# Attention in a decoder step: the second four heads of each block are normalised on GpSimd instead of ScalarE

## What is computed

```python
s = jnp.einsum('bnqhgd,bnkhd->bnhgqk', qb, kb).astype(jnp.float32) * (HEAD_B ** -0.5)
s = jnp.where(valid[None, :, None, None], s + bias[None], NEG_INF)
m = jnp.maximum(s.max(-1), sink)
p = jnp.exp(s - m[..., None])
p = p / (p.sum(-1) + jnp.exp(sink - m))[..., None]
return jnp.einsum('bnhgqk,bnkhd->bnqhgd', p, vb.astype(jnp.float32))
```

## Time and profile before

| | |
|---|---|
| median of 3 runs | 1639.69 us (1639.18 to 1644.08) |
| the profiled execution | 1647.76 us, its span 1645.9 us |
| TensorE, matmuls | 1460.3 us busy, 89% of the span |
| TensorE, weight loads | 893.1 us, 54% |
| VectorE | 642.4 us, 39% |
| ScalarE | 365.8 us, 22% |
| GpSimd | 206.2 us, 13% |

### The profile page before, as it was taken

How to read it: one execution, slowest core, us unless ns; L and a number is a source line. 1 busy time by engine, 2 the same in 40 slices (tenths; PEclk the granted TensorE clock), 3 DMA queues, 4 the chain that set the end, 5 groups by cost and what they waited for, 6 DMA issues and landing times. The chain is left out here.

```text
span 1645.9 us, 26231 instructions
## 1 busy us (share of the span) xinstructions
PE 1460.3 (89%) x10107; PEld 893.1 (54%) x10108; DVE 642.4 (39%) x1022; ACT 365.8 (22%) x788; POOL 206.2 (13%) x263
## 2 busy tenths in 40 slices
PE   7999999966779997999839999994995699999968
PEld 5566666645668885454424444443794344444423
DVE  1122553069246552777451111114795311111127
ACT  1333110056523332111101111111231111111111
POOL 4000000000054321110011010105000111010040
PEclk7999999988689999999959999996797699999989
DMA  6573110040020003000368887776005778786453
GB/s 193 124 278 135 39 26 26 0 114 21 9 53 4 4 4 115 26 26 26 112 218 305 289 296 270 247 267 217 27 5 207 251 256 306 270 285 222 152 213 122
DMA packets 137055, 236.96 MB, mean 144 GB/s; under 512 B 20178, under 2 KB 100035, under 8 KB 136682
## 3 DMA queue, kind: packets, MB, share of 16 engines
q1 hardware_dynamic: 113458, 151.01, 28.9%
q0 software_dynamic: 16880, 60.49, 10.0%
q10 hardware_dynamic: 6624, 24.12, 3.6%
HBM read 178.92 MB, written 58.21 MB: 144 GB/s over the span
## 5 line engine op out<-in xcount | busy, mean ns | idle before, releaser
L2259 PE MATMUL ex_pb<-ew_w_gate_up,ex_xT 128*128 x736 | 329.8, 601 | 6.1 <-issue 3.7
L298 PE MATMUL pj_pb<-pj_xT,pj_w 128*128 128x348 f32 (+3 forms) x960 | 284.0, 457 | 0.4 <-ACT pj_xT L322 0.4
L298 PEld LDWEIGHTS pj_pb<-pj_xT,pj_w 128*128 128x128 f32 (+1 forms) x960 | 179.6, 187 | 102.6 <-issue 2.6
L2259 PEld LDWEIGHTS ex_pb<-ew_w_gate_up,ex_xT 128*128 128x128 f32 x736 | 138.0, 193 | 165.0 <-issue 164.1
L2242 PE MATMUL ex_pb<-ew_w_down,ex_hiddenT 128*128 x368 | 165.7, 593 | 3.4 <-ACT ex_hiddenT L2329 3.4
L2452 DVE TENSOR_TENSOR ex_hidden<-ex_hidden,ex_pb 128x256 f32<-128x256 f32 x46 | 19.4, 421 | 324.5 <-ACT ex_hidden L2324 324.5
L2242 PEld LDWEIGHTS ex_pb<-ew_w_down,ex_hiddenT 128*128 128x128 f32 x368 | 66.3, 190 | 69.9 <-issue 69.9
L2447 DVE COPY ex_y_rows<-ex_pb 128x512 f32<-128x512 f32 x46 | 31.8, 692 | 134.5 <-PE ex_pb L2242 134.5
L430 DVE SCALAR_TENSOR_TENSOR mixed<-pj_pb,v_mu,mixed 128x347 f32<-128x347 f32 (+3 forms) x42 | 24.0, 572 | 147.6 <-ACT mixed L372 147.5
L2324 ACT ACTIVATE ex_hidden<-ex_pb 128x256 f32<-128x256 f32 x46 | 17.8, 386 | 261.3 <-PE ex_pb L2259 261.3
L1890 PE MATMUL mo_pb<-late_rows,projected_qkv 128*128 128x512 f32 (+1 forms) x144 | 66.7, 608 | 0.0
(11 more groups left out here) (414 smaller groups left out, 2072.8 us busy)
## 6 DMA issues: line engine op xcount, KB each, us to landing
ew_w_gate_up<-in_w_ex_gate SPq DMA_DIRECT2D x32, 1024.0 KB, 7.8
ew_w_gate_up<-in_w_ex_up SPq DMA_DIRECT2D x32, 1024.0 KB, 10.9
ew_w_down<-in_w_ex_down SPq DMA_DIRECT2D x32, 1024.0 KB, 12.8
scratch_slots_out<-ex_y_rows ACTq DMA_DIRECT2D x46, 512.0 KB, 4.9
scratch_slots_out<-pj_tmp POOLq DMA_DIRECT2D x4, 4096.0 KB, 15.9
scratch_x_stored<-x_rows SPq DMA_DIRECT2D x16, 512.0 KB
pj_w<-in_w_in SPq DMA_DIRECT2D x7, 1024.0 KB, 8.4
minus_kk_then_y<-in_x_prompt SPq DMA_DIRECT2D x8, 512.0 KB, 5.4
```

The lines of the kernel that those rows point to most:

```text
L298: last = nc.tensor.matmul(product(at)[:, 0:tn], w[:, s % NW, k, c0:c0 + mrows], xT[:, k, x0:x0 + tn], start=(k == 0), stop=(k == KD - 1))
L2259: last = mm(pb[:, 2 + u, :], xT[:, u, k, :], w[:, k, :], start=(k == 0), stop=(k == KD - 1))
```

## The change

The constant H_ACT becomes H_DVE, with the same value 4. ScalarE's `normalise` and its call are gone. GpSimd gets a list of its own: for each block it waits for `inv` and multiplies heads 4 to 7 in place by their factors, in one instruction over 4x256 columns (4x128 in block 0), of the same form as VectorE's L811. TensorE's transposes 2 and 3 wait for GpSimd's `prob_p` in place of `prob_a`.

```diff
             def transposes(n, mm):
-                pe.wait_ge(q["prob_v" if 2 * mm < H_ACT else "prob_a"], n + 1)
+                pe.wait_ge(q["prob_v" if 2 * mm < H_DVE else "prob_p"], n + 1)
...
-            def normalise(n):
-                lo, u = (0 if n else P), n % 3
-                act.wait_ge(q["inv"], n + 1)
-                for h in range(H_ACT, H):
-                    last = nc.scalar.activation(s[:, u, h, lo:2 * WIN], s[:, u, h, lo:2 * WIN], ACT.Identity,
-                                                scale=st[:, u, 5, h:h + 1])
-                last.then_inc(q["prob_a"], 1)
-
...
             for n in range(NT):
                 if n + 1 < NT:
                     exps(n + 1)
-                normalise(n)
                 if n:
                     act.wait_ge(q["o"], n)
...
+        @block.gpsimd
+        def _(pool):
+            for n in range(NT):
+                lo, u = (0 if n else P), n % 3
+                pool.wait_ge(q["inv"], n + 1)
+                nc.gpsimd.tensor_tensor(s[:, u, H_DVE:H, lo:], s[:, u, H_DVE:H, lo:],
+                                        st[:, u, 5, H_DVE:H].unsqueeze(2).to_broadcast([P, H - H_DVE, 2 * WIN - lo]), ALU.mult)\
+                    .then_inc(q["prob_p"], 1)
+
```

More of the change, by code:

```diff
@@ L485, in attend @@
     VW = 384
-    H_ACT = 4
+    H_DVE = 4
     with Memory(nc, "at") as m:
@@ L522, in attend @@
         pb = m.psum("pb", [P, 8, 512])
-        names = ("sink v_tr v_cp bias_rd sc masked neg ex inv prob_v prob_a ptr pcp o y out k0 chain"
+        names = ("sink v_tr v_cp bias_rd sc masked neg ex inv prob_v prob_p ptr pcp o y out k0 chain"
                  " k_in v_in s_in kt ktc qc ssc sscc tr mx sex spr tr2 tr2c so sy"
@@ L810, in normalise @@
                 dve.wait_ge(q["inv"], n + 1)
-                tt(s[:, u, 0:H_ACT, lo:], s[:, u, 0:H_ACT, lo:],
-                   st[:, u, 5, 0:H_ACT].unsqueeze(2).to_broadcast([P, H_ACT, 2 * WIN - lo]), ALU.mult).then_inc(q["prob_v"], 1)
+                tt(s[:, u, 0:H_DVE, lo:], s[:, u, 0:H_DVE, lo:],
+                   st[:, u, 5, 0:H_DVE].unsqueeze(2).to_broadcast([P, H_DVE, 2 * WIN - lo]), ALU.mult).then_inc(q["prob_v"], 1)
             HH = HR // 2
```

## The result

The changed kernel took 1652.8 us (median of 6 runs, 1649.17 to 1654.69), the kernel before 1644.64 beside it (6 runs, 1639.18 to 1648.15). The two medians lie 8.2 us apart, a ratio of 1.0050; the comparison on record puts the ratio of the runs at 1.0039, 95% interval 1.0022 to 1.0056, which is 6.4 us. By either the changed kernel is slower, by 0.4 to 0.5%. Forecast were 1644.4 and a range up to 1648.5, so the measured time lies outside it. The profiled execution took 1651.56 us (span 1649.8), against 1647.76 (1645.9): 3.8 us more.

What follows compares the result with a forecast made beforehand. VectorE was taken to bound blocks 1 to 4 of `attend`, with ScalarE's normalisation on the path only in block 6. Hold-ups of 6.3 us less 1.6 gave +4.7 on the median 1639.69: 1644.4 us, range 1638.5 to 1648.5.

Steps and rivals of the forecast that it cites:

- Who is first: At each block's L811: VectorE starts 0.04 us after L809, GpSimd needs 0.15, so L811 goes first and loses nothing.
- rival 2: GpSimd gets the port before L811, holding it up 1.86 us in five blocks; +8.7 us, 1648.4; chance 0.08.
- GpSimd's 1.89 us: Length of the added GpSimd multiplication per block, 1024 columns at 1.67 ns a column; 1.04 us in block 0.
- wrong if the GpSimd rows are far from 1.9 us: Sign in the profile after: new GpSimd rows should last 1.9 us, else the prediction is wrong.
- Who gets in between: After L811, waiting GpSimd gets the port at the instruction's end, ahead of a VectorE instruction that is ready.
- The four hold-ups: Blocks 1 to 4: VectorE's two-input SBUF instruction after L811 late by 1.68, 1.68, 1.28, 1.68 us; 6.3 in all.
- block 5's is covered: Block 5: L876 is late by 1.7 us, covered by VectorE's 3.51 us of idle time until 416.82.
- The tail: Block 6: without ScalarE's normalisation its copy, and TensorE behind it, start 1.6 us earlier, all of it gain.
- The clock: TensorE's granted clock, mainly in the tail: taken as 0, range -2 to +1.5 us; as a rival, chance 0.08.
- VectorE keeps the port: Blocks 1 to 4: VectorE holds it while its next instruction needs it; +1.6 us, 1641.3; chance 0.14.
- nothing collides: One GpSimd instruction leaves room for VectorE, so only the gain in block 6 is left; -1.6 us, 1638.1; chance 0.08.
- the last line of the sum: Whole program: the +4.7 us inside the stage is added to the median of 1639.69, giving 1644.4.

Runs made afterwards that it cites:

- b4_at_reduce: Changed kernel, but in blocks 1 to 4 GpSimd waits for one more VectorE semaphore, to start beside a reduce; 1650.26 us, ratio 1.002 to the kernel before.
- b5_split: Changed kernel with GpSimd's multiplication cut in four, one instruction for each head (256 columns); 1648.81 us in a single run.
- a2_last_three: Against the kernel before: GpSimd normalises the second four heads in blocks 5 to 7 alone, ScalarE in blocks 0 to 4; 1639.99 us, ratio 0.9962.
- c1_last_three: GpSimd in blocks 5 to 7 alone, measured again on another chip; ratio 0.9989 to the kernel before.
- a4_spare_mult: Kernel before, plus a GpSimd multiplication of a spare tile that nobody reads, released by the same semaphore; 1652.43 us, ratio 1.0043.
- c3_spare_memset: Kernel before, plus two GpSimd memsets of a spare tile, which write SBUF but read none; 1645.82 us, ratio 1.001.

## Why the prediction was right and wrong

**Who is first.** Right, with less to spare than reckoned. L811 starts 0.05 us before GpSimd's row and keeps 1.22. GpSimd's row stands 0.08 us behind the end of L809 (360.67 + 0.20, then 360.95), where the prediction reckoned with 0.15 and saw rival 2 below 0.04.

**GpSimd's 1.89 us.** Right as a duration: where it waits for no port, in b4_at_reduce, its rows have 1.89. The rows of the changed kernel have 2.93, and by the prediction's own sign ("wrong if the GpSimd rows are far from 1.9 us") that would have spoken against it. The sign was badly chosen, and so was the sentence that the rows would start 1 us after L811: the record begins with the instruction's release, not with the port, so 2.93 is 1.04 of waiting behind L811 and 1.89 of work. Its end, 360.95 + 2.93 = 363.88, is 2.98 after L811's start, as against 2.95 reckoned.

**Who gets in between.** Right, and by the prediction's own word the step with least behind it, so part of this is luck. VectorE's next instruction was ready and still waited. b5_split shows the turn-taking four times in a row.

**The four hold-ups.** 1.70, 1.70, 1.32 and 1.70 against 1.68, 1.68, 1.28 and 1.68; in sum 6.4 against 6.3. That the blocks in between have no slack held in three profiles to 0.01 us. That block 5's is covered held as well, with 1.88 us left of 3.51.

**The tail.** 1.5, 1.8 and 1.5 us against 1.6.

**The clock.** From block 6 to L709 the changed kernel took 19.29, 20.89 and 19.51 us against 20.13: -0.8 to +0.8, inside the bounds of -2 to +1.5; the prediction took 0. That TensorE isn't the bound in blocks 1 to 4 was true by 0.6 us only; a2_last_three, c1_last_three and b4_at_reduce all ran into it.

**Not foreseen.** The barrier behind the stage takes 0.4 us more (7.54 against 7.14) in all three profiles and in b4_at_reduce, but not in b5_split or with GpSimd in some of the blocks. It lies ahead of the first instructions of the next stage: GpSimd's L1101 starts 2.26 us after L709 instead of 1.85. No run tells why.

**The rivals.** That VectorE keeps the port, that GpSimd is first, that nothing collides: each would have shown in the rows after, and none did. a4_spare_mult and c3_spare_memset show that it is the reading.

**The step that failed** is the last line of the sum: "the change is a difference inside one stage, so I add it to the median: 1644.4". The difference, +4.7, was right to within what 116 runs can tell (+4.2 with 1.4 either way). The number it was added to was not. The median of 1639.69 rested on three runs; all 86 runs of the kernel before, these three among them, have a mean of 1645.3 and go from 1635.9 to 1654.1, and only 11 of them are below 1640, two of the three among these. Of the 8.4 us between 1644.4 and the measured 1652.8 the anchor makes up 5.6. The difference takes off 0.5. The rest, some 3 us, is that the first comparison's own six runs of the changed kernel lie above its mean of 1649.6 over 30; why they do, no run shows. The profiled run, at 1647.76, stood 8.1 us above the median and outside the range of the three. I saw that and explained it away, where it should have widened the range. Added to the profiled run's own time the sum is 1652.5, but that this comes so close to 1652.8 is luck too: the profiled run stood 2.4 us above the mean. A range that held the anchor's own uncertainty, from 1639.7 + 4.7 to 1647.8 + 4.7 and the terms' 3 us on top, would have reached 1655.

## What to carry to other kernels

Moving work to GpSimd is not moving it off VectorE's books: look at what VectorE has next in that moment. If VectorE's next instruction reads two tensors from SBUF, it waits until a GpSimd instruction that reads SBUF is almost done, whatever its own size (1.7 us for one of 8 columns). Move work only where the engine that is freed is on the path and VectorE is idle: here that is block 6. The version with GpSimd in blocks 5 to 7 alone gave 0.9962 and 0.9989, a mean of 1641.8 us over 22 runs, below both kernels; in block 6 alone it gave 0.9994, which can't be told from no change. And where a profiled run stands outside the few timed ones, give the anchor a range of its own.

## What was not expected of the hardware

- VectorE and GpSimd take turns at the port, instruction by instruction, even if either has the next one ready. Over blocks 1 to 4, four GpSimd instructions of 256 columns a block cost VectorE 3.2 us, one of 1024 a block 6.4.
- A GpSimd row that waits for the port is recorded from its release: 2.93 us for 1.89 of work. A VectorE row holds its wait as well: 1.86 us for an instruction of 0.16.
- GpSimd's writes alone leave a TENSOR_TENSOR as it is (1.22) but held two TENSOR_SCALARs from SBUF up by 0.23 us each.
- One kernel's runs spread over 18 us, 1.1%, and the part of the program behind the stage over almost 5 us between profiles. So an effect of 0.3% can be read to 0.01 us from a segment that one engine bounds (57.27, 57.27 and 57.28 us), but from the time of the whole only with dozens of runs.
